# Expert layer of a two-block transformer, head by head: choice beside the query projection, u and v rows interleaved, 12 of 16 v rows summed by TensorE

## What is computed

```python
def peer(xn, wq, subkeys, u, v):
    q = (xt @ wq).reshape(T, PEER_HEADS, 2, PEER_QDIM // 2)       # 8 heads, 2 sides of 128
    s1 = einsum('thd,nd->thn', q[:, :, 0], subkeys[0])            # 128 scores a side
    s2 = einsum('thd,nd->thn', q[:, :, 1], subkeys[1])
    v1, i1 = top_k(s1, 16); v2, i2 = top_k(s2, 16)
    cand = v1[..., :, None] + v2[..., None, :]                    # 256 sums
    sc, ci = top_k(cand, 16)
    idx = i1[ci // 16] * 128 + i2[ci % 16]                        # 16 experts a head
    gate = softmax(sc)
    h = gelu(einsum('cd,chkd->chk', xc, u[ic]))
    return einsum('chk,chkd->cd', gate * h, v[ic])
```

## Time and profile before

| | |
|---|---|
| median of 3 runs | 3805.93 us (3803.12 to 3809.45) |
| profiled execution, its own time | 3796.77 us |
| span of the profiled execution | 3795.1 us |
| PE busy | 2150.0 us (57%) |
| DVE busy | 1895.6 us (50%) |
| POOL busy | 1240.8 us (33%) |
| ACT busy | 345.1 us (9%) |

### The profile page before, as it was taken

One profiled execution on the slowest core, in us unless ns is written; L12 is line 12 of the kernel. 1 busy time (PEld: TensorE's weight loads), 2 busy tenths in 40 slices (PEclk: granted clock), 3 DMA queues, 4 the chain that ended last, 5 costly groups with the idle time before them and its releaser, 6 DMA issues.

```text
span 3795.1 us, 26301 instructions
## 1 busy us (share of the span) xinstructions
PE 2150.0 (57%) x8630; PEld 1471.9 (39%) x8630; DVE 1895.6 (50%) x2283; ACT 345.1 (9%) x717; POOL 1240.8 (33%) x697
## 2 busy tenths in 40 slices
PE   5999648999999999979988989100000000000000
PEld 3444635488888864434488659100000000000000
DVE  5662554310000000010045214899988888888887
ACT  1000341110110100010034210000000000000000
POOL 2110100000000000000000000677788888888886
PEclk9999768999999999989978999655555555555555
DMA  9996103644444444435400247999899999999998
GB/s 381 396 401 237 59 0 123 225 150 152 147 154 155 151 147 149 151 130 192 134 26 1 67 147 264 368 407 385 358 398 387 384 378 393 366 390 385 379 386 327
DMA packets 236363, 932.82 MB, mean 246 GB/s; under 512 B 18011, under 2 KB 33555, under 8 KB 164115
## 3 DMA queue, kind: packets, MB, share of 16 engines
q0 software_dynamic: 99840, 637.57, 42.0%
q1 hardware_dynamic: 136197, 294.44, 22.6%
q10 hardware_dynamic: 272, 0.13, 0.0%
HBM read 928.89 MB, written 2.15 MB: 245 GB/s over the span
## 4 chain that ended last, share of the span: by engine, by line
PE 52%; DVE 22%; DMA 11%; POOL 7%; issue 5%; ACT 2%; DVEq 0%; SPq 0%; POOLq 0%; ACTq 0%
PE ps L1095 16%; PE ps L809 14%; DVE x L1904 9%; PE ps L1108 8%; DVE ring L1866 4%; DVE proj L1866 4%; POOL ring L463 4%; PE ps L1243 3%; DMA ring<-in_w_in 3%; DMA ring<-in_peer_u,proj 3%; POOL proj L463 2%; PE ps L841 2%; DMA proj<-in_peer_v,proj 2%; DMA ring<-in_peer_v,proj 2%; DMA arena<-in_w_mod 1%
## 5 line engine op out<-in xcount | busy, mean ns | idle before, releaser
L454 POOL COPY proj<-proj 128x8 int32 x64 | 112.5, 1758 | 1739.6 <-DVE proj L1839 1697.0
L1095 PE MATMUL ps<-hT,ring 128*128 128x256 f32 x2816 | 608.0, 379 | 1.4 <-ACT hT L491 1.4
L1095 PEld LDWEIGHTS ps<-hT,ring 128*128 128x128 f32 x2816 | 535.0, 190 | 74.3 <-issue 1.7
L809 PE MATMUL ps<-ring,hT 128*128 128x512 f32 (+2 forms) x960 | 381.3, 558 | 13.5 <-DMA ring<-in_w_in 13.5
L1904 DVE SCALAR_TENSOR_TENSOR x<-proj,x 128x2048 f32<-128x2048 f32 x128 | 301.5, 2356 | 73.1 <-DMA proj<-in_peer_v,proj 58.5
L1904 DVE SCALAR_TENSOR_TENSOR x<-ring,proj,x 128x2048 f32<-128x2048 f32 x128 | 301.3, 2354 | 25.8 <-DVE x L1904 9.1
L1108 PE MATMUL ps<-ring,arena 128*128 128x512 f32 x704 | 304.1, 595 | 2.7 <-ACT arena L674 2.7
L1866 DVE CUSTOM_DVE_ANT_0 proj<-proj,yT 128x2048 f32<-128x2048 f32 x128 | 288.5, 2289 | 25.6 <-DMA proj<-in_peer_u,proj 22.6
L1866 DVE CUSTOM_DVE_ANT_0 ring<-ring,yT 128x2048 f32<-128x2048 f32 x128 | 289.6, 2291 | 18.0 <-DMA ring<-in_peer_u,proj 17.0
L463 POOL DMA_INDIRECT ring<-in_peer_v,proj x128 | 278.8, 2178 | 39.0 <-issue 39.0
L463 POOL DMA_INDIRECT proj<-in_peer_v,proj x128 | 268.9, 2101 | 58.6 <-issue 29.3
(11 more groups left out here) (402 smaller groups left out, 2253.3 us busy)
## 6 DMA issues: line engine op xcount, KB each, us to landing
arena<-in_w_mod POOLq DMA_DIRECT2D x96, 1024.0 KB
ring<-in_w_in SPq DMA_DIRECT2D x52, 1024.0 KB, 13.2
ring<-in_ffn_w_gate SPq DMA_DIRECT2D x44, 1024.0 KB, 5.0
ring<-in_ffn_w_up SPq DMA_DIRECT2D x44, 1024.0 KB, 5.0
ring<-in_ffn_w_down SPq DMA_DIRECT2D x44, 1024.0 KB, 4.8
ring<-in_w_out SPq DMA_DIRECT2D x32, 1024.0 KB, 6.3
ring<-in_peer_wq SPq DMA_DIRECT2D x32, 1024.0 KB, 5.1
ring<-in_w_in SPq DMA_DIRECT2D x16, 960.0 KB, 16.5
```

The costliest lines, as they stand in the source:

```text
L454: pool_eng.tensor_copy(expert_now[:, half, :], expert[:, t, bass.ds(i * (2 * ROWS) + ROWS * half, ROWS)]).then_inc(sem("experts_now"), 1)
L809: ins = pe.matmul(ps[:, 2 * (b % 2) + t, 0:w], lhs[:, KS * s + k, P * t:P * (t + 1)], ring[:, s, k, 0:w], start=(s == 0 and k == 0), stop= ...
L1095: ins = pe.matmul(ps[:, 4 * m + f, 0:T], ring[:, s, k, P * f:P * (f + 1)], hT[:, KS * s + k, :], start=(s == 0 and k == 0), stop=(s == SLO ...
```

## The change

The layer is done head by head; `g` counts the 16 pairs of tile and head.

- **Projection.** Both tiles are multiplied at once, 256 columns a matmul, so `peer_wq` is read once, in four blocks of two heads. PE scores head h-1 after the first quarter of head h's matmuls. ACT copies the scores of tile 0 into `score` and those of tile 1 into `later`, which lies in the used half of `gates`.
- **Choice.** `choose_head(t, h)` does one head of one tile. For tile 0 it runs as the scores of each head come; from head 2 on two dots of head 0 follow each choice. For tile 1 it runs in the first eight turns of the main loop.
- **Rows.** POOL issues 16 u rows of head g+1, then 16 v rows of head g, and so on, and reads the expert numbers where they lie, without a copy. The slots lie in `proj` and `arena` and not in `ring`. Each slot has its own semaphore `free{s}`.
- **v rows.** Of every four v rows DVE adds the last (rows 3, 7, 11, 15, `add_rows`). The other 12 (`BY_PE`) are summed by PE: ACT makes for each a 128 x 128 diagonal matrix of its weights (`diag`), and four matmuls of 512 columns add the weighted row into four banks of PSUM, where it stays until the tile is done. `join` then adds the four banks to `x`.
- **End.** The norm of tile 0 and its store come in the turns g = 7 to 9, those of tile 1 at the end.

The diff, cut to its core (what stands for the rest is shorter buffers and names):

```diff
-for _n, _c in (("in1", 12), ("out1", 4), ("up", 22), ("down", 11), ("in2", 7), ("out2", 4), ("wq", 8)):
+for _n, _c in (("in1", 12), ("out1", 4), ("up", 22), ("down", 11), ("in2", 7), ("out2", 4), ("wq", 4)):
...
+    peer = carve(arena[:], {"q": (2, 2, T), "score": (4, 2, P), "sum": (1, TOP * TOP), "hot": (TOP, TOP), "val": (2, TOP), "at_f": (2, TOP),
+                            "hi_f": (1, TOP), "lo_f": (1, TOP), "e1": (1, TOP), "e2": (1, TOP)})
+    later = gates[:, 0, :].rearrange("p (c n) -> p c n", n=P)
...
-    row_slots = [flat_proj[:, D * s:D * (s + 1)] for s in range(4)] + [ring[:, s].rearrange("p k n -> p (k n)") for s in range(4)]
...
+    GS = NT * HEADS
+    U_AT = lambda g: max(2 * g - 1, 0)
+    V_AT = lambda g: min(2 * g + 2, 2 * GS - 1)
+    BY_PE = tuple(s for s in range(TOP) if s % 4 != 3)
+    v_added = lambda g: at(f"free{BY_PE[-1] % ROWS}", 2 * V_AT(g) + 3)
+    diag = hT[:].rearrange("p k t -> p (k t)")[:, 0:2 * len(BY_PE) * P].rearrange("p (a s m) -> p a s m", a=2, m=P)
+    row_slots = [flat_proj[:, D * s:D * (s + 1)] for s in range(4)] + [arena[:, 4608 + D * s:4608 + D * (s + 1)] for s in range(4)]
...
-        for t in range(NT):
-            stream(w1v["peer_wq_2"], BLK["wq"] + 4 * t, 4, 0)
+        stream(w1v["peer_wq_2"], BLK["wq"], 4, 0)
...
-        for phase, table in enumerate((a["peer_u_2"], a["peer_v_2"])):
-            for t in range(NT):
-                pool_eng.wait_ge(*at("experts", t + 1))
-                base = PICKS * (NT * phase + t)
-                with pool_eng.Fori(0, PICKS // (2 * ROWS)) as i:
-                    for half in range(2):
-
-                        pool_eng.wait_ge(*at("row_used", i * (2 * ROWS) + (base + ROWS * half + 1)))
-                        pool_eng.tensor_copy(expert_now[:, half, :], expert[:, t, bass.ds(i * (2 * ROWS) + ROWS * half, ROWS)]).then_inc(sem("experts_now"), 1)
...
-                            pool_eng.wait_ge(*at("row_used", i * (2 * ROWS) + (base + ROWS * half + s + 1)))
-                            pool_eng.sem_inc(sem("pool_turn"), 1)
-                            pool_eng.indirect_dma_start(row_slots[s], None, table, bass.IndirectOffsetOnAxis(expert_now[:, half, s:s + 1], 0))\
-                                    .then_inc(sem(f"row{s}"), 16)
+        def gather(table, g, seg):
+            for r in range(TOP):
+                s = r % ROWS
+                pool_eng.wait_ge(*at(f"free{s}", 2 * seg + r // ROWS + 1))
+                pool_eng.indirect_dma_start(row_slots[s], None, table, bass.IndirectOffsetOnAxis(expert[:, 0, TOP * g + r:TOP * g + r + 1], 0))\
+                        .then_inc(sem(f"row{s}"), 16)
+
+        for g in range(GS):
+            for u in ((0, 1) if g == 0 else (g + 1,)):
+                if u < GS:
+                    pool_eng.wait_ge(*at("experts", u + 1))
+                    gather(a["peer_u_2"], u, U_AT(u))
+            gather(a["peer_v_2"], g, V_AT(g))
...
-        for t in range(NT):
-            with act.Fori(0, 4) as i:
-                act.wait_ge(*at("unit_used", i * SLOTS + SLOTS * (BLK["wq"] + 4 * t + 1)))
-                act.copy(peer["q"][:, bass.ds(i * 4, 4), P * t:P * (t + 1)], ps[:, 0:4, 0:P]).then_inc(sem("wq_out"), 1)
...
-            act.activation(best, best, ACT.Exp).then_inc(sem("best_exp"), 1)
-        for t in range(NT):
-            act.wait_ge(*at("h_done", t + 1))
-            act.activation(peer["h"][:, t, :], peer["h"][:, t, :], ACT.Gelu_apprx_tanh).then_inc(sem("h_gelu"), 1)
-        act.wait_ge(*at("x_done", 5))
-        norm(5, scaled=False)
...
+        def best_exp(g):
+            act.wait_ge(*at("best_shift", g + 1))
+            w = peer["weight"][:, 0, TOP * g:TOP * (g + 1)]
+            act.activation(w, w, ACT.Exp, accum_out=peer["total"][:, 0, g:g + 1]).then_inc(sem("best_exp"), 1)
...
+        for h in range(HEADS):
+            if h % 2:
+                act.wait_ge(*at("unit_used", SLOTS * (BLK["wq"] + h // 2 + 1)))
+            else:
+                act.wait_ge(*at("wq_even", h // 2 + 1))
+            pair = 2 * (h % 2)
+            act.copy(peer["q"][:, h % 2], ps[:, pair:pair + 2, 0:T]).then_inc(sem("wq_out"), 1)
+            act.wait_ge(*at("keys_scored", h + 1))
+            if h >= 4:
+                act.wait_ge(*at("experts", h - 3))
+            if h == 0:
+                act.wait_ge(*at("xs_scaled", 1))
+            scored = ps[:, 4 + h % 2, :].rearrange("p (t s n) -> p t s n", t=NT, s=2)
+            act.copy(peer["score"][:, h % 4], scored[:, 0]).then_inc(sem("score_out"), 1)
+            act.copy(later[:, 2 * h:2 * h + 2, :], scored[:, 1]).then_inc(sem("later_out"), 1)
+            if h:
+                best_exp(h - 1)
+        best_exp(HEADS - 1)
+        for g in range(GS):
+            act.wait_ge(*at("h_done", g + 1))
+            h = peer["h"][:, 0, TOP * g:TOP * (g + 1)]
+            act.activation(h, h, ACT.Gelu_apprx_tanh).then_inc(sem("h_gelu"), 1)
+            if 1 <= g <= HEADS:
+                best_exp(HEADS + g - 1)
+            act.wait_ge(*at("weights", g + 1))
+            if g >= 2:
+                act.wait_ge(*v_added(g - 2))
+            for j, s in enumerate(BY_PE):
+                ins = act.activation(diag[:, g % 2, j, :], ident, ACT.Copy, scale=peer["weight"][:, 0, TOP * g + s:TOP * g + s + 1])
+            ins.then_inc(sem("diag_out"), 1)
+            if g == HEADS + 1:
+                last_norm(0)
+        last_norm(1)
...
-        for t in range(NT):
-            with pe.Fori(0, 4) as i:
-                pe.wait_ge(*at("wq_out", i + (4 * t + 1)))
-                for s in range(SLOTS):
-                    pe.wait_ge(sem(f"slot{s}"), i * 16 + 16 * (BLK["wq"] + 4 * t + 1))
-                    for k in range(KS):
-                        for f in range(4):
-                            ins = pe.matmul(ps[:, f, 0:P], ring[:, s, k, P * f:P * (f + 1)], hT[:, KS * s + k, P * t:P * (t + 1)],
-                                            start=(s == 0 and k == 0), stop=(s == SLOTS - 1 and k == KS - 1))
...
+        for h in range(HEADS):
+            if h >= 2:
+                pe.wait_ge(*at("wq_out", h - 1))
+            for s in range(SLOTS):
+                if h % 2 == 0:
+                    pe.wait_ge(*at(f"slot{s}", 16 * (BLK["wq"] + h // 2 + 1)))
+                for k in range(KS):
+                    for f in range(2):
+                        col = P * (2 * (h % 2) + f)
+                        ins = pe.matmul(ps[:, 2 * (h % 2) + f, 0:T], ring[:, s, k, col:col + P], hT[:, KS * s + k, :],
+                                        start=(s == 0 and k == 0), stop=(s == SLOTS - 1 and k == KS - 1))
+                if h % 2:
...
+                elif s == SLOTS - 1:
+                    ins.then_inc(sem("wq_even"), 1)
+                if s == 0 and h:
+                    score_head(h - 1)
+        score_head(HEADS - 1)
+
+        pe.wait_ge(*at("wq_out", HEADS))
+        pe.wait_ge(*at("later_out", HEADS))
+        for g in range(GS):
+            t, h = g // HEADS, g % HEADS
+            pe.wait_ge(*at("diag_out", g + 1))
+            for j, s in enumerate(BY_PE):
+                pe.wait_ge(*at(f"row{s % ROWS}", 16 * (2 * V_AT(g) + s // ROWS + 1)))
+                for n in range(4):
+                    ins = pe.matmul(ps[:, 4 * t + n, :], diag[:, g % 2, j, :], row_slots[s % ROWS][:, NB * n:NB * (n + 1)],
+                                    start=(h == 0 and j == 0), stop=(h == HEADS - 1 and s == BY_PE[-1]))
+                ins.then_inc(sem(f"free{s % ROWS}"), 1)
...
+        def choose_head(t, h):
+
+            scores = peer["score"][:, h % 4] if t == 0 else later[:, 2 * h:2 * h + 2, :]
+            val, best = peer["val"], peer["best"][:, HEADS * t + h, :]
+            top16(2, lambda c: scores[:, c, :], lambda c: val[:, c, :], lambda c: at_u[:, c, :])
...
+            top16(1, lambda c: sums, lambda c: best, lambda c: pick_u[:, 0, :])
             for s, (op, arg, f, e) in enumerate(((ALU.logical_shift_right, 4, "hi_f", "e1"), (ALU.bitwise_and, 15, "lo_f", "e2"))):
...
+            g = HEADS * t + h
+            link(vec.tensor_copy(expert[:, 0, TOP * g:TOP * (g + 1)], peer["e1"][:, 0, :]), "experts")
+            link(vec.tensor_tensor(peer["weight"][:, 0, TOP * g:TOP * (g + 1)], best, best[:, 0:1].to_broadcast([P, TOP]), ALU.subtract), "best_shift")
...
+        def dot_row(g, s):
+            arrived(U_AT(g), s)
+            slot = row_slots[s % ROWS]
+            vec.tensor_tensor_reduce(slot, slot, xs[:, g // HEADS], 1.0, 0.0, ALU.mult, ALU.add, peer["h16"][:, 0, s:s + 1]).then_inc(sem(f"free{s % ROWS}"), 1)
+
+        def dots_done(g):
+            vec.wait_ge(*at(f"free{ROWS - 1}", 2 * U_AT(g) + 3))
+            link(vec.tensor_copy(peer["h"][:, 0, TOP * g:TOP * (g + 1)], peer["h16"][:, 0, :]), "h_done")
+
+        def add_rows(g):
+            t = g // HEADS
+            for s in range(TOP):
+                if s not in BY_PE:
+                    arrived(V_AT(g), s)
```

(70 more changed lines are left out.)

139 lines of the change are left out of this document (43 added, 96 removed).

## The result

The changed kernel takes 3665.23 us in the median of four runs (3652.14 to 3668.89); the kernel before, on the same chip, 3806.89 us (3803.12 to 3809.45). The ratio is 0.9619, with a 95% interval of 0.9604 to 0.9635: 142 us less. The prediction of 3698 us is 33 us too high, and the result lies inside the forecast's own range of 3660 to 3735, 5 us above its lower end. The profiled execution took 3663.8 us with a span of 3662.1.

The account below looks back on a forecast made before the run. Close limits of DMA (2.5 us a row), DVE (2.45) and POOL (up to 2.8) bound the kernel. Start 2415, gathers 1247, tile 0's store 3 and end 22 make 3687 us, 3698 at the median; range 3660 to 3735.

Parts of the forecast that it names:

- the distance from span to median: Median of the runs over the profiled span: 10.8 us in the kernel before, added to 3687 to give 3698.
- Start: Up to row 24's landing, the 25th gather: at about 2415 us instead of 2449.7, 35 us earlier.
- The choice: Tile 0's experts chosen head by head on DVE: 9.8 us a head, 14.2 with two dots, under the projection's 14.7.
- Pace: The 487 gathers after row 24: 2.56 us each at DMA's rate, bounds 2.52 and 2.64, instead of 2.727; 81 us gained.
- the pace stays: Rival for the gathers: they remain at 2.73 us a row, only the earlier start counts, 3779 us at the median; chance 0.11.
- the reading of 358 GB/s as a limit: Skill page's HBM limit a core, giving 2.93 us a row; the trace disagreed with 416, so it got no own chance.
- POOL: Gather issue: without 64 copies of 2.9 us, at most 65 us for a head's rows, where DMA needs 80.
- DVE: Dots, tile 1's choice and four v rows: 56 us a head in the first eight heads, under DMA's 80.
- PE: Twelve v rows a head: 41.4 us plus 3 for the cold start, 44.4 in all, costed at nothing.
- TensorE becomes the bound: Rival for the v rows: without full clock twelve rows take 83 us, about 114 a head, 4250 at the median; chance 0.12.
- The cover: Slack before a v row's slot is due again: 18.3 us needed of 20.2, so 2 us.
- End: After the last landing: PE ends about 8 us behind, then `join` and one tile's norm, about 22 us instead of 17.5.

## Why the prediction was right, step by step

The span was forecast as 2415 + 1247 + 3 + 22 = 3687 and is 2420 + 1221 + 21 = 3662. Of the 33 us by which the median was missed, 25 are in this sum and 8 in the distance from span to median, taken from the kernel before as 10.8 and now 3.1.

*Start.* 2415 against 2420. The mechanism was right: 36 us by the run without it. That run is not the baseline of the 35 that were forecast, since its row 24 leaves at 2445.1 and that of the kernel before at 2440.9; against the kernel before, the start gained 28 to 30. The choice was mis-sized. It takes 14.83 - 4.42 = 10.4 us a head, not 9.8, and with two dots it is over the projection's 14.7, so that DVE sets the pace of this stage, where I had put it just under. Head 1's first dot starts at 2409.7, not 2405.

*Pace.* 2.56 us a row against 2.507: the 487 rows and the store took 29 us less than their 1250, where the start took 5 more and the end 1 less. The term was mis-sized toward the stretch with POOL's stops. DMA alone sets the pace, and it gives 420 GB/s without a break, more than the best window of the earlier trace rows; I had kept 1.6% over that window for hiccups, and there were none. So the pace lies just outside the bounds of 2.52 to 2.64, and the result below the 3668 that the sum gives for the range's fastest pace, 2.50; that it is still inside 3660 to 3735 owes something to the width of the range. The rival "the pace stays" falls. So does the reading of 358 GB/s as a limit, now over 1232 us: the row of the Trainium skill (DMA: Bandwidth & Descriptors, Specifications) gives half of a stack's 716 GB/s, a share for two cores, and here one core ran alone.

*POOL.* That it leaves the path was right: 50 of 80 us busy a head. That its copies were what the kernel before paid for was right in kind (87 us for them and their loop, more than the 81 that I gave to the whole of the pace), but the prediction did not divide the pace among the copies, the order and PE. In steps that were run: copies 87, head start 36, and 19 for all else together. Of this rest only PE's part was run by itself, 43 us; so the order of the rows, the choice head by head and the query weights read once would together lose about 24. That is an estimate by subtraction, and no run has any of these three by itself.

*DVE.* 56.4 busy of 80 in the first eight heads, 56 forecast.

*PE.* 43 to 44.5 us a head against 44.4, as the cold start costs 1.6 to 3.1 us where 3 was forecast. It works at the high clock, with 0.94 granted in its stretch, so the rival "TensorE becomes the bound" falls, though the clock does drop to 0.50 in each idle time. The cover held: at a DMA share of 1.01 no slot comes too late. How near the edge lies was seen with all 16 rows on PE (+136 us) and with half rows, where PE and the refill take 77 us of DMA's 80: the cover is about 3 us a head. The prediction's 2 us were per slot, and came out otherwise. I had added the median landing, 8.8 us, to PE's lag of 9.1. Now the lag at the end is 8.4 and the median landing 11.9, together 20.3 of 20.1 us for eight rows, and still nothing is late. A landing while DMA is full contains the time in DMA's own queue, so it is not a delay that must fit ahead of the slot's turn; that reading is argued from these numbers, and no run took it apart.

*End.* 21.1 us behind the last landing against 22; PE's lag of 8.4 was forecast at 8.

## What to carry to other kernels

Put each engine's time per turn beside that of the transfers, but also the chains that run through the ring of buffers (engine time plus the time to fill the ring again): they bind long before the engine is full, as with 740 of 1140 us here. When two streams share the DMA engines, look at their packets' sizes: the one with small packets gets the small share, and it needs a gate if the other can wait. An issuing engine that is only just in time hides how much each small instruction on it costs: 13 us or 47 us for the same copies, by what DVE does beside them.

## What the runs showed of the hardware that I had not expected

- Gathers of 8 KB rows at random places ran at 420 GB/s for 1232 us, on one core.
- 2 KB pieces of a load beside 8 KB pieces of gathers got 88 of 413 GB/s, packet for packet, and a 1 MiB load took 29 us instead of about 5 from issue to landing.
- A gather's issue on POOL took 0.94 us beside an idle or briefly busy DVE, 1.91 beside back-to-back dots, and 2.2 to 2.9 us in places beside DVE's long instructions with eight v sums a head. It kept step with DVE: the gathers started 2.21 us apart while the dots did (from 2413 us on in the changed kernel), and 2.49 apart while the dots waited for landings (from 2405 us on in the run without early gathers). A copy of eight numbers took 2.12 us beside DVE's choice, and 1.0 in the mean of 60.
- TensorE, idle for 37 us in every turn with its clock at 0.50, lost 1.6 to 3.1 us of 43 to 44.5 to the cold start.
